# One-hot gate products of a PEER layer in bf16: the gate in three parts, the masks with four tokens innermost

## The reference, cut to what matters

```
q = (xb @ w_pq).reshape(PEER_BLOCK, P_HEADS, 2, P_HALF)
sc = jnp.einsum('thpc,hpkc->thpk', q, sub_keys)
sv, si = lax.top_k(sc, TOPK)
...
eid = jnp.take_along_axis(cid, fi, axis=-1)
g = jax.nn.softmax(fv.astype(jnp.float32), axis=-1)
ue = jnp.take(u_experts, eid, axis=0)
ve = jnp.take(v_experts, eid, axis=0)
a = jax.nn.gelu(jnp.einsum('thkd,td->thk', ue, xb), approximate=False)
return jnp.einsum('thk,thkd->td', g * a, ve)
```

## Time and profile before

| | |
|---|---|
| median of 3 runs | 2202.97 us |
| the profiled execution | 2208.66 us |
| its span, first to last instruction | 2207.0 us |
| TensorE busy | 2152.3 us (98%), 14712 matmuls |
| VectorE busy | 1683.5 us (76%) |
| ScalarE busy | 1098.2 us (50%) |
| mean granted TensorE clock | 0.990 of full |

### The profile page before, as it was taken

How to read it: one execution, slowest core, us unless ns; L and a number is a source line. 1 busy time by engine, 2 the same in 40 slices (tenths; PEclk the granted TensorE clock), 3 DMA queues, 4 the chain that set the end, 5 groups by cost and what they waited for, 6 DMA issues and landing times. The chain is left out here.

```text
span 2207.0 us, 46403 instructions
## 1 busy us (share of the span) xinstructions
PE 2152.3 (98%) x14712; PEld 2005.6 (91%) x14712; DVE 1683.5 (76%) x2461; ACT 1098.2 (50%) x1651; POOL 367.5 (17%) x344
## 2 busy tenths in 40 slices
PE   6999999999999999999989999999999999999998
PEld 6999899999999988888889989999999998888886
DVE  6665658999999687677775746599999996667776
ACT  6445454444444454554464545444444445554454
POOL 3110110000000155334230101100000002333442
PEclk9999999999999999999998999999999999999999
DMA  5444466765555677777644444567655557777774
GB/s 192 153 144 152 145 207 213 230 203 178 173 174 176 224 260 242 239 242 243 223 135 135 150 166 168 188 225 231 194 175 176 171 176 256 244 240 242 241 240 164
DMA packets 173982, 437.49 MB, mean 198 GB/s; under 512 B 19360, under 2 KB 84896, under 8 KB 172752
## 3 DMA queue, kind: packets, MB, share of 16 engines
q1 hardware_dynamic: 173232, 432.09, 59.5%
q0 software_dynamic: 672, 4.39, 0.6%
HBM read 399.70 MB, written 36.70 MB: 198 GB/s over the span
## 5 line engine op out<-in xcount | busy, mean ns | idle before, releaser
L746 DVE TENSOR_TENSOR w_lo<-raw,w_hi 128x1024 fp32r<-128x1024 f32 x680 | 844.7, 1245 | 401.8 <-ACT w_hi L714 183.1
L1143 PE MATMUL ps<-act_hi,w_hi 128*128 128x256 f32 x2880 | 829.6, 288 | 3.2 <-DVE act_lo L797 1.9
L1143 PE MATMUL ps<-act_lo,w_hi 128*128 128x256 f32 x2880 | 819.8, 285 | 0.0
L1143 PE MATMUL ps<-act_hi,w_lo 128*128 128x256 f32 x2880 | 819.8, 285 | 0.0
L1143 PEld LDWEIGHTS ps<-act_hi,w_hi 128*128 128x128 f32 x2880 | 558.1, 194 | 5.5 <-DVE act_lo L797 2.3
L1143 PEld LDWEIGHTS ps<-act_hi,w_lo 128*128 128x128 f32 x2880 | 558.2, 194 | 0.1
L1143 PEld LDWEIGHTS ps<-act_lo,w_hi 128*128 128x128 f32 x2880 | 557.5, 194 | 0.0
L714 ACT ACTIVATE w_hi<-raw 128x1024 fp32r<-128x1024 f32 x248 | 263.1, 1061 | 323.5 <-PE ps L1403 311.7
L1403 PE MATMUL ps<-w_hi,act_hi 128*128 128x512 f32 x1000 | 389.2, 389 | 2.0 <-DVE act_lo L1107 2.0
L1403 PE MATMUL ps<-w_lo,act_hi 128*128 128x512 f32 x1000 | 389.0, 389 | 0.0
L1403 PE MATMUL ps<-w_hi,act_lo 128*128 128x512 f32 x1000 | 389.0, 389 | 0.0
(11 more groups left out here) (248 smaller groups left out, 2105.9 us busy)
## 6 DMA issues: line engine op xcount, KB each, us to landing
raw<-slabs SPq DMA_DIRECT2D x684, 512.0 KB, 3.6
h_park<-h_out SPq DMA_DIRECT2D x256, 128.0 KB, 1.7
h_in<-h_park SPq DMA_DIRECT2D x250, 128.0 KB, 3.7
memT<-mem POOLq DMA_DIRECT2D x2, 1024.0 KB, 6.6
skT<-sub_keys POOLq DMA_DIRECT2D x2, 1024.0 KB, 8.0
x_park<-xT SPq DMA_DIRECT2D x2, 1024.0 KB, 5.4
xT<-x_park SPq DMA_DIRECT2D x2, 1024.0 KB, 8.4
xT<-x SPq DMA_DIRECT2D x1, 1024.0 KB, 5.0
```

Source lines behind the costliest of these rows:

```text
L746: nc.vector.tensor_tensor(w_lo[:, j].rearrange("p k c -> p (k c)"), raw[:, j, :], w_hi[:, j].rearrange("p k c -> p (k c)").bitcast(FP32), ...
L1143: last = nc.tensor.matmul(ps[:, j, 0:T], w[:, j, k, :], a[:, k, :], start=(k == 0 and i == 0), stop=(k == KB - 1 and i == 2))
```

## The change

The masks and the gate go from 4-byte to 2-byte elements, and the tokens of a group become the innermost axis of every mask.

- `iota` is bf16 and repeats each position for four tokens; `row_is`, `hot_col` and `hot_row` are laid out [position, token].
- The gate is split into three bf16 parts (each the rest of what the parts before hold) where it was two float32r parts. `hot_row` grows from 1024 to 1536 elements.
- `rowT`, `colT` and `gate2` become one tensor `picks` [128, 5, 256] in bf16; filling it takes five VectorE instructions where it was four, with one more temporary (`g_rest`).
- A group's products are 4 x 3 = 12 matmuls in bf16 where they were 8 in float32r. Weights and moving operand are read with a step of four elements (8 bytes).

```diff
-        hot_col = at("hot_col", x_at, [P, 4, P], F32R)
-        hot_row = at("hot_row", x_at + 2048, [P, 2, 4, P], F32R)
+        hot_col = at("hot_col", x_at, [P, P, 4], BF16)
+        hot_row = at("hot_row", x_at + 2048, [P, PARTS, P, 4], BF16)
...
-        rowT = sb("rowT", [P, T])
-        colT = sb("colT", [P, T])
-        gate2 = sb("gate2", [P, 2, T], F32R)
+
+        picks = at("picks", top[0], [P, 2 + PARTS, T], BF16)
...
-            nc.gpsimd.iota(iota[:], [[1, P]], base=0, channel_multiplier=0,
+            nc.gpsimd.iota(iota[:], [[1, P], [0, 4]], base=0, channel_multiplier=0,
...
-                                                        (b_f, iota, ALU.is_equal, cols, col_f)):
+                                                        (b_f, iota[:, :, 0], ALU.is_equal, cols, col_f)):
...
-                step.mark(nc.vector.tensor_copy(rowT[:], ps[:, 4, 0:T]))
-                step.mark(nc.vector.tensor_copy(colT[:], ps[:, 4, T:2 * T]))
-                step.link(nc.vector.tensor_copy(gate2[:, 0], ps[:, 5, 0:T]))
-                step.link(nc.vector.tensor_tensor(gate2[:, 1], ps[:, 5, 0:T], gate2[:, 0].bitcast(FP32), ALU.subtract))
+                step.mark(nc.vector.tensor_copy(picks[:, 0:2], ps[:, 4, :].rearrange("p (i t) -> p i t", i=2)))
+                step.link(nc.vector.tensor_copy(picks[:, 2], ps[:, 5, 0:T]))
+                step.link(nc.vector.tensor_tensor(g_rest[:], ps[:, 5, 0:T], picks[:, 2], ALU.subtract))
+                step.link(nc.vector.tensor_copy(picks[:, 3], g_rest[:]))
+                step.link(nc.vector.tensor_tensor(picks[:, 4], g_rest[:], picks[:, 3], ALU.subtract))
...
-                    nc.vector.tensor_tensor(row_is[:], iota[:].unsqueeze(1).to_broadcast([P, 4, P]),
-                                            rowT[:, ds(n * 4, 4)].unsqueeze(2).to_broadcast([P, 4, P]),
+                    nc.vector.tensor_tensor(row_is[:], iota[:],
+                                            picks[:, 0, ds(n * 4, 4)].unsqueeze(1).to_broadcast([P, P, 4]),
...
-                    nc.vector.tensor_tensor(hot_col[:], iota[:].unsqueeze(1).to_broadcast([P, 4, P]),
-                                            colT[:, ds(n * 4, 4)].unsqueeze(2).to_broadcast([P, 4, P]),
+                    nc.vector.tensor_tensor(hot_col[:], iota[:],
+                                            picks[:, 1, ds(n * 4, 4)].unsqueeze(1).to_broadcast([P, P, 4]),
                                             ALU.is_equal).then_inc(hot_col_ready, 1)
-                    nc.vector.tensor_tensor(hot_row[:], row_is[:].unsqueeze(1).to_broadcast([P, 2, 4, P]),
-                                            gate2[:, :, ds(n * 4, 4)].bitcast(FP32).unsqueeze(3).to_broadcast([P, 2, 4, P]),
+                    nc.vector.tensor_tensor(hot_row[:], row_is[:].unsqueeze(1).to_broadcast([P, PARTS, P, 4]),
+                                            picks[:, 2:2 + PARTS, ds(n * 4, 4)].unsqueeze(2).to_broadcast([P, PARTS, P, 4]),
...
-                        for part in range(2):
-                            last = nc.tensor.matmul(ps[:, 4 + s, i * P:(i + 1) * P], hot_col[:, i, :],
-                                                    hot_row[:, part, i, :], start=(part == 0), stop=(part == 1))
+                        for part in range(PARTS):
+                            last = nc.tensor.matmul(ps[:, 4 + s, i * P:(i + 1) * P], hot_col[:, :, i],
+                                                    hot_row[:, part, :, i], start=(part == 0), stop=(part == PARTS - 1))
```

More of the change, by code:

```diff
@@ L100 @@
 H_SLOTS = 2
+PARTS = 3
 TEMPS = 88
@@ L176, in trunk @@
         tri = sb("tri", [P, P])
-        iota = sb("iota", [P, P])
+        iota = at("iota", top[0], [P, P, 4], BF16)
+        top[0] += P * 4 * 2
         cand_at = sb("cand_at", [P, TOPK])
@@ L182, in trunk @@
         wif_lo = sb("wif_lo", [P, KB, 8], F32R)
-        row_is = at("row_is", par_at, [P, 4, P], BF16)
+        row_is = at("row_is", par_at, [P, P, 4], BF16)
         assert top[0] - par_at >= 4 * P * 2
-        rowT = sb("rowT", [P, T])
-        colT = sb("colT", [P, T])
-        gate2 = sb("gate2", [P, 2, T], F32R)
+        picks = at("picks", top[0], [P, 2 + PARTS, T], BF16)
+        top[0] += (2 + PARTS) * T * 2
         gated_at = top[0]
@@ L262, in trunk @@
         struck = tmp("struck", 109, [P, 2, NKEYS])
+        g_rest = tmp("g_rest", 104, [P, T])
         h_park = nc.dram_tensor("h_park", (NKEYS, P, T), FP32, kind="Internal").ap()
```

## The result

The change makes the kernel slower: 2272.45 us (median of 4 runs, 2270.78 to 2275.35) against 2203.52 (median of 4 in the same comparison), a ratio of 1.031 with a 95% interval of 1.0288 to 1.0331. The forecast was 2188.3 us, in a range of 2176 to 2263, so the time lies above the range as well.

What follows compares the result with a forecast made beforehand. TensorE was taken to bound the gate stages, VectorE a close second. 0.4 us more before the stage and 15.1 us gained made -14.7 us, from 2202.97 to 2188.3 us; range 2176 to 2263.

Steps and rivals of the forecast that it cites:

- the price of one bf16 product: Gate stage, TensorE: load and stream together taken as 0.060 us, between bounds of 0.058 and 0.112; break-even at 0.071.
- That rival: No faster load at all, or the stream at half rate: twelve gate products at 0.112 us, 2261 us; chance 0.12.
- the prediction's own formula for the turn: Gate stage, TensorE: slab product's first load at 0.11 + 11 x 0.060 + 0.01 = 0.78 us, was 0.90; 15.1 us gained.
- What bounds the kernel: Gate stages: TensorE sets the end with a 3.77 us turn, VectorE close behind; a loss needs only one to get longer.
- VectorE's part: Gate-stage masks: packed operands pass two elements per cycle, so VectorE's turn is 2.96 us, under TensorE's 3.65.
- The unpacked case: Gate-stage masks stay at one element per cycle: VectorE bounds with a turn of 4.30 us, 2271 us; chance 0.08.
- The faster weight load: Gate products, TensorE: bf16 weight loads last about 0.14 us where 0.19 stood.
- The pace of load and matmul pairs: Gate products: the skill's about 81 ns per 128-column pair would give 2217 us, its word against this change.
- The seam: Last bf16 gate product to float32r slab load: only 0.06 us of 0.112 hides; 0.12 us less per turn, not 0.18.
- Before the stage: Filling picks takes 2.6 us, 1.0 more; first group ready 0.2 us later per layer; 0.4 us counted over both layers.
- hot_row alone does not pack: Gate-stage masks: row_is times gate stays unpacked, VectorE's turn 3.76 us, about 2203 us; part of no change, chance 0.08.
- the pace lies between 0.071 and 0.112: Gate products: bf16 pairs don't reach the stream's pace; at 0.086 us 2224 us, span 2207 to 2230; chance 0.12.

## Why the prediction was wrong

The step that failed is the price of one bf16 product, p = 0.060 us. It was derived from two rows, the stream of 128 columns and the weight load ahead of a transpose, and both were of packed operands; the run with both operands packed shows that for those it was right (0.056). The 8-byte step of the moving operand was named in the bounds ("unless the step of 8 bytes costs something") and in a rival ("It decides already if only the stride halves the moving read (2 x 0.058 = 0.116)"), then given a chance of 0.12; the forecast itself put the step at nothing, without a reason. The price measured 0.118, and the runs with one packed operand put the difference to the moving read: 0.116 with its step, 0.056 without. Put into the prediction's own formula for the turn, 0.11 + 11 x 0.118 + 0.01 = 1.42 us against 0.90, it gives 0.52 us, 66 us in all; measured 68 in the gate stages and 69 in all. The formula's total comes out, its parts don't: the first gate load starts 0.01 us ahead of its matmul and not 0.11, and from it to the slab product's first load it is 1.29 us.

That rival's price of 2261 us was still 11 us short: it had been worked out at 0.112, the load pace of before, though the same paragraph had 0.116 for the halved stream. At 0.118 it would have been 2269. The range ended 2 us above the rival, at 2263; with 2269 in it, it would have ended at 2271, still just under the measured 2272.

Point by point:

- **What bounds the kernel** was right: TensorE with VectorE close behind, and a loss if only one of them got longer.
- **VectorE's part** was right in size. row_is and hot_col 0.42 us, hot_row 0.95 (forecast 0.42 and 0.96). The unpacked case had 4.30 us and 2271; the run with tokens outermost measured 4.33 and 2270.8.
- **The faster weight load** was right in kind, and the load was faster than the forecast 0.14: 0.098 us packed instead of 0.19, as the rule in the Trainium skill, TensorE: Matmul & The Clock Gate, section Weight-path perf modes, has it for non-FP32 weights; with a step of 8 bytes 0.115, and 0.117 in the changed kernel, still faster than before. The rule speaks of the weights only, and the moving operand decided.
- **The pace of load and matmul pairs**, which by section Back-to-back issue gap of that page in the Trainium skill is about 81 ns, was 56 ns here in a group of twelve packed pairs; the measurement decides.
- **The seam** between the types was forecast at 0.06 us a turn (0.12 us less, not 0.18). With packed operands the turn is 3.61 us, 0.16 less than before, where 12 x 0.056 in place of 8 x 0.112 alone would be 0.22 less: 0.06 us. The prediction put it to the float32r load that hides only in part; a price of the switch between the types itself is not told apart from that.
- **Before the stage** the sign was wrong, by a small sum. 0.4 us more of waiting was counted; in layer two TensorE stood without a matmul for 1.01 us before and for under 0.1 us now. Filling `picks` took 2.27 us from the first copy to the end of the last subtraction, 0.7 more than before and not 1.0, and the first hot_row ended 6.62 us after the start of the first copy, where it was 6.68 and 0.2 more was forecast. TensorE's last slab matmul ahead of the group started 6.3 us after that copy instead of 5.4; why, the runs leave open.

```profile
1614.17 0.69 DVE L1074 CAST picks<-ps 128x512 bf16<-128x512 f32 x1 [1.61 <-PE ps L1374]
...
1616.01 0.43 DVE L1078 TENSOR_TENSOR picks<-g_rest,picks 128x256 bf16<-128x256 f32 x1
...
1619.84 0.95 DVE L1097 TENSOR_TENSOR hot_row<-row_is,picks 128x1536 bf16<-128x1536 bf16 x1
```

- **The rivals** in which hot_row alone does not pack, or the pace lies between 0.071 and 0.112, did not occur.

The general error was to take the change's two layouts as one matter. The argument "runs of 8 bytes" was made for VectorE, for which it held, and the same 8 bytes were a step, not a run, for TensorE.

## What to carry to other kernels

When a layout is changed for one engine, write down for every other reader of the tile what its innermost step becomes in bytes, and price that. Here a moving operand of TensorE kept its pace up to a step of 4 bytes (0.057 us for 128 columns, 0.056 packed) and took twice as long at 8. Where two engines want opposite layouts, look for the smallest interleave that both accept: pairs of bf16 elements gave VectorE its two per cycle and TensorE its full pace, and turned 3.1% lost into 0.8% gained.

## What was not expected of the hardware

- The moving read's cost by the step: 0.056 to 0.057 us for 128 columns at steps up to 4 bytes, 0.089 at 6, 0.118 at 8, 0.230 at 16, and 0.233 at 32. The Trainium skill, SBUF — State Buffer, section Door 1: The DMA port swizzle, says that two accesses to each 16-byte line are enough for full bandwidth; the measurement decides, and on TensorE's moving read two ran at half the pace, two to three (6 bytes) at 0.63 of it, and four at the full one.
- float32r goes by bytes as well: a step of two elements doubled it, 0.12 to 0.23 us for 256 columns.
- The slowest moving reads came with a lower clock: at steps of 16 and 32 bytes the granted clock of the gate stages fell to 0.95 and 0.96 on average, where it was 1.00 at 2 to 8 bytes (one execution of each).
- A bf16 load of 128 strided weights lasted 0.115 us against 0.098 packed, and was hidden but for the first of a group.
- GpSimd's iota took 1.19 us for 512 bf16 elements where 128 in float32 had taken 0.24; at most 1 us had been counted. The type is not what made it longer: 128 bf16 elements took the same 0.24 us in the kernel with tokens outermost, while in the kernel with token pairs, where each position is repeated twice, 256 took 1.52. Both slow ones write each position more than once; these are single records. It ended ahead of the first load all the same, as the changed kernel's start shows:

```profile
2.01 1.19 POOL L432 IOTA iota<- 128x512 bf16 x1
...
7.34 1.06 ACT L570 ACTIVATE w_hi<-raw 128x1024 fp32r<-128x1024 f32 x1 [2.54 <-DMA raw<-slabs]
```
